# Latent rotations on GpSimd, second vectors between dense tiles, centred retention values and shorter sums in a sixteen-step transformer kernel

## The reference

```python
# layers 0 and 1 of the first block
shift_m, scale_m, gate_m, shift_f, scale_f, gate_f = split(silu(c) @ ada_w + ada_b, 6)
h = rms_norm(x, g) * (1 + scale_m) + shift_m
y = attn_hybrid_mixer(h) if layer == 0 else retention_mixer(h)
x = x + gate_m * y
...
# layer 0: 8 stick-breaking heads, 8 softmax ("moba") heads whose q and k are rotated
qm, km = rotary(q[:, 8:], pos), rotary(k[:, 8:], pos)
...
# layer 1: retention, 4 heads, dk 256, dv 512
o = (q k^T * decay) v
mu = mean(o); var = mean((o - mu) ** 2)
o = (o - mu) * rsqrt(var + 1e-5) * gn_gain
y = (silu(g) * o) @ w_o
# layers 2 and 3: h @ w_in, then a convolution branch, a latent attention of 8 heads
# (q and k normed per head and rotated), a dilated attention of 24 heads, a gated merge
```

## Time and profile before

| | us |
|---|---|
| median of 3 runs | 1530.87 |
| lowest and highest | 1525.58 and 1535.09 |
| the profiled execution | 1537.26 |
| its span, first to last instruction | 1535.5 |
| around the span | 1.8 |

### The profile page before, as it was taken

One profiled execution on the slowest core, in us unless ns is written; L12 is line 12 of the kernel. 1 busy time (PEld: TensorE's weight loads), 2 busy tenths in 40 slices (PEclk: granted clock), 3 DMA queues, 4 the chain that ended last, 5 costly groups with the idle time before them and its releaser, 6 DMA issues.

```text
span 1535.5 us, 30455 instructions
## 1 busy us (share of the span) xinstructions
PE 1492.0 (97%) x11736; PEld 1405.6 (92%) x11736; DVE 1034.7 (67%) x1821; ACT 853.2 (56%) x1438; POOL 85.5 (6%) x136
## 2 busy tenths in 40 slices
PE   8988999999999999999999999999999999999998
PEld 7777999999989999999998888889999888988998
DVE  2687688899694566555665756886666675687664
ACT  3446566544445655555565665555556666555553
POOL 0110000011000000000020000220000000021000
PEclk9999999999999999999999999999999999999999
DMA  9776488899674355565663454336666345433663
GB/s 375 264 252 191 138 274 288 287 359 334 204 275 139 111 169 161 188 185 185 190 223 122 140 163 153 111 93 183 194 189 213 108 142 171 145 97 97 193 195 122
DMA packets 81326, 292.56 MB, mean 191 GB/s; under 512 B 9200, under 2 KB 10480, under 8 KB 81088
## 3 DMA queue, kind: packets, MB, share of 16 engines
q1 hardware_dynamic: 67408, 244.03, 48.8%
q0 software_dynamic: 11792, 42.77, 8.2%
q10 hardware_dynamic: 2016, 4.21, 0.8%
HBM read 289.92 MB, written 1.05 MB: 189 GB/s over the span
## 4 chain that ended last, share of the span: by engine, by line
PE 81%; DVE 11%; ACT 4%; issue 3%; DMA 0%; SPq 0%; DVEq 0%; ACTq 0%
PE G L484 19%; PE G L485 19%; PE G L486 19%; DVE wlo L1522 4%; PE G L543 2%; PE G L545 2%; PE G L544 2%; ACT whi L1071 2%; PE G L565 1%; PE O L1017 1%; PE Tp L874 1%; PE S L986 1%; DVE aw L1530 1%; PE Tp L827 1%; PE S L600 1%
## 5 line engine op out<-in xcount | busy, mean ns | idle before, releaser
L1522 DVE TENSOR_TENSOR wlo<-raw,whi 128x1024 fp32r<-128x1024 f32 x444 | 546.7, 1233 | 309.1 <-ACT whi L1071 306.0
L484 PE MATMUL G<-h,whi 128*128 128x256 f32 x2096 | 600.2, 286 | 6.0 <-DVE at L2087 2.8
L1071 ACT ACTIVATE whi<-raw 128x1024 fp32r<-128x1024 f32 x444 | 468.7, 1057 | 241.2 <-PE G L486 179.3
L485 PE MATMUL G<-h,whi 128*128 128x256 f32 x2096 | 585.4, 279 | 0.0
L486 PE MATMUL G<-h,wlo 128*128 128x256 f32 x2096 | 585.3, 279 | 0.0
L484 PEld LDWEIGHTS G<-h,whi 128*128 128x128 f32 x2096 | 398.9, 190 | 15.3 <-issue 6.0
L485 PEld LDWEIGHTS G<-h,whi 128*128 128x128 f32 x2096 | 397.5, 190 | 1.7 <-issue 0.5
L486 PEld LDWEIGHTS G<-h,wlo 128*128 128x128 f32 x2096 | 396.9, 189 | 0.0
L1530 DVE CUSTOM_DVE_ANT_0 aw<-aw,cs,cols 128x1024 f32<-128x1024 f32 x80 | 102.3, 1279 | 0.0
L484 PE MATMUL G<-ah,whi 128*128 128x256 f32 x352 | 98.0, 278 | 0.0
L485 PE MATMUL G<-ah,whi 128*128 128x256 f32 x352 | 98.0, 278 | 0.0
(11 more groups left out here) (336 smaller groups left out, 2298.8 us busy)
## 6 DMA issues: line engine op xcount, KB each, us to landing
raw<-in_w SPq DMA_DIRECT2D x444, 512.0 KB, 3.7
aw<-in_ada POOLq DMA_DIRECT2D x80, 512.0 KB, 5.4
adaw<-in_ada SPq DMA_DIRECT2D x8, 1024.0 KB, 17.6
sn<-in_uq ACTq DMA_DIRECT2D x2, 768.0 KB, 4.4
x<-in_x SPq DMA_DIRECT2D x1, 1024.0 KB, 5.4
pt<-in_ukv ACTq DMA_DIRECT2D x2, 512.0 KB, 5.5
out<-x SPq DMA_DIRECT2D x4, 256.0 KB, 2.3
cs<-in_crow SPq DMA_DIRECT2D x1, 512.0 KB, 3.3
```

Of the source, the lines that this page charges most:

```text
L484: pe.matmul(o, wh, mv[:, 0:T], start=(k == 0), stop=False)
L485: pe.matmul(o, wh, mv[:, T:2 * T], start=False, stop=False)
L1071: act.activation(whi[:, s, :], raw[:, s, :], ACT.Copy).then_inc(w_hi, 1)
L1522: dve.tensor_tensor(wlo[:, s, :], raw[:, s, :], whi[:, s, :], ALU.subtract).then_inc(w_lo, 1)
```

## The change

1. **Rotation on GpSimd.** `rope_moba` leaves DVE. GpSimd runs the same twelve instructions between its transfers: six behind the transfer r = 5 (after b3's tile is carried off), six behind r = 9 (after b7's). PE waits for them on `mro_ready`. The transfers r = 6 to 8 now stand behind the first six, r = 10 and all later ones behind the second six.
2. **Start.** c comes as one row of 4 KB, ACT takes its silu on one partition, and PE spreads it to 128 by two matmuls of 512 columns and one row (`cs_wide`), which ACT copies to `cs` (`cs_copied`; DVE's stage loop waits for that). `x` comes ahead of `cols`. Seven small tables (780 KB) move from ACT's queue, where ACT issued them ahead of its first squares, to SyncE's, behind `adaw`. The second half's two rows and two columns are issued between the dense tiles k = 0, 1, 2, 3 of the first. The unused matmuls go from 76 to 65 (16, 2, 6, 3, 30, 8).
3. **Retention.** `v` is centred per token and head before it is used: ACT's copies of the token tiles also give row sums (`accum_out`), and DVE subtracts the mean (`centre`, at b20, 24, 28, 32: one small addition, one scalar_tensor_tensor of 128 x 1024). The mean of `o` is then zero, and the mean's matmuls, copy and subtraction go. The squares of four tiles are added by DVE to one (two instructions), so PE sums one tile, not four. Part 3 of head n moves from 36 + 4n to 35 + 4n, so none is behind b47. PE's outputs wait for `rv_ready` too.
4. **Late run.** In `run_late` the wait for the second PSUM bank stands ahead of the second tile's matmuls, no longer ahead of both.
5. **Layers 2 and 3.** The lora sums are split over j = 1 and 2, what follows is one tile later on all engines, and the heads' transposes start at j = 19 instead of 16; the last three stand among the value blocks.
6. **Head loop.** In the two steps with two dense tiles (i = 1 and i = 10) DVE carries off the first of them ahead of `minima(i)`.

The diff, cut to what the prediction speaks of:

```diff
+RET_PARTS = {}
 for _n in range(4):
-    for _part, _b in enumerate((32, 33, 34, 36)):
-        if _b + 4 * _n < 48:
-            RET_PARTS.setdefault(_b + 4 * _n, []).insert(0 if _part == 0 else 1, (_n, _part))
+    for _part, _b in enumerate((32, 33, 34, 35)):
+        RET_PARTS[_b + 4 * _n] = (_n, _part)
...
         @block.gpsimd
+            def rope_moba(n):
+                A, B = mqk[:, 4 * n:4 * n + 4:2, :], mqk[:, 4 * n + 1:4 * n + 4:2, :]
+                RA, RB = mro[:, 4 * n:4 * n + 2, :], mro[:, 4 * n + 2:4 * n + 4, :]
+                for s in range(4):
+                    pool.wait_ge(slot_free[s], 1 + n)
+                pool.tensor_tensor(RA, A, cos, ALU.mult)
+                chain.link(pool.tensor_tensor(rtmp[:, :, :], B, sin, ALU.mult))
+                chain.link(pool.tensor_tensor(RA, RA, rtmp[:, :, :], ALU.subtract))
...
                 pool.dma_start(aw[:, r % ADA_SLOTS, :], a["ada"][16 + r]).then_inc(ada_raw[r % ADA_SLOTS], 16)
+                if r in (5, 9):
+                    if r == 5:
+                        pool.wait_ge(in_att, 64)
+                    rope_moba(r // 4 - 1)
...
             def run_late(b, g, k_of, early, moving, each_k, b4=0, g4=0):
-                for m in range(2):
-                    pe.wait_ge(slot_free[(g + m - 2) % 4], taken(g + m - 2) + g4)
...
+                    if ks[0] == 0:
+                        pe.wait_ge(slot_free[(g + m - 2) % 4], taken(g + m - 2) + g4)
...
+            run_first([(0, n) for n in range(4)])
+            ada_rows(1, 0)
+            run_first([(1, n) for n in range(4)])
+            ada_cols(1, 0)
+            run_first([(2, n) for n in range(4)])
+            ada_rows(1, 1)
+            run_first([(3, n) for n in range(4)])
+            ada_cols(1, 1)
+            keep_busy(8, Tp[:, 0, :])
...
             def ret_out(hh):
                 pe.wait_ge(r_pt, hh + 1)
+                pe.wait_ge(rv_ready, hh + 1)
...
-            def ret_sum(src, sem_, n):
+            def ret_sum(hh):
                 slot = use_t()
-                pe.wait_ge(sem_, n)
-                for m in range(4):
-                    ins = pe.matmul(Tp[:, slot, 0:T], ones[:, :], sq[:, src + m, :], start=(m == 0), stop=(m == 3))
-                ins.then_inc(t_done, 1)
+                pe.wait_ge(r_added, hh + 1)
+                pe.matmul(Tp[:, slot, 0:T], ones[:, :], sq[:, 4, :], start=True, stop=True).then_inc(t_done, 1)
...
-                    if j >= 16:
-                        mla_transposes(j - 16)
+                    if j >= 19:
+                        mla_transposes(j - 19)
...
-                if b in (5, 9):
-                    rope_moba(b // 4 - 1)
...
                 for i in range(18):
+                    first = TAKEN[i][:1] if len(TAKEN[i]) > 1 else []
+                    for j in first:
+                        head_block(j)
                     if i < 16:
                         minima(i)
-                    for j in TAKEN[i]:
+                    for j in TAKEN[i][len(first):]:
                         head_block(j)
```

More of the change, by code:

```diff
@@ L97 @@
 L1_S = len(ATT_S)
-L1_T = 8 + 8
+L1_T = 8 + 4
 L1_O = 8
@@ L573, in run_two, with run_first @@
                     ins.then_inc(blk_done, 1)
-            def run_first(half):
-                tiles = [(k, n) for k in (range(0, 4) if half == 0 else range(4, 6)) for n in range(4)]
-                if half:
-                    tiles += [(k, n) for n in range(4) for k in range(6, 8)]
+            def run_first(tiles):
                 for k, n in tiles:
@@ L691, in _ @@
             pe.wait_ge(silu_c, 1)
-            for half in range(2):
-                for vec in range(2):
-                    idle = S[:, 0, :] if half == 0 else Tp[:, 0, :] if vec else O
-                    keep_busy(4, idle)
-                    ada_rows(half, vec)
-                    keep_busy(3, idle)
-                    ada_cols(half, vec)
-                keep_busy(6 if half else 22, idle)
-                run_first(half)
+            keep_busy(2, S[:, 0, :])
+            ada_rows(0, 0)
+            for n in range(2):
+                ins = pe.matmul(G[:, n, :], ones[0:1, :], cs[0:1, 512 * n:512 * n + 512], start=True, stop=True)
+            ins.then_inc(cs_wide, 1)
+            ada_cols(0, 0)
+            keep_busy(6, S[:, 0, :])
+            ada_rows(0, 1)
+            keep_busy(3, S[:, 0, :])
+            ada_cols(0, 1)
+            keep_busy(30, S[:, 0, :])
+            pe.wait_ge(cs_copied, 1)
+            run_first([(0, n) for n in range(4)])
[7 more added lines that the diff above has]
+            keep_busy(8, Tp[:, 0, :])
+            run_first([(k, n) for k in range(4, 6) for n in range(4)] + [(k, n) for n in range(4) for k in range(6, 8)])
             def sb_scores(hh):
@@ L899, in _, with lora_sums @@
                     block_u(j)
-                def lora_sums():
+                def lora_sums(tiles):
                     pe.wait_ge(csq_ready, l + 1)
-                    for tiles in ((0, 1), (2,)):
-                        slot = use_t()
-                        for k in tiles:
-                            ins = pe.matmul(Tp[:, slot, 0:T], ones[:, :], csq[:, k, :], start=(k == tiles[0]),
-                                            stop=(k == tiles[-1]))
-                        ins.then_inc(t_done, 1)
+                    slot = use_t()
+                    for k in tiles:
+                        ins = pe.matmul(Tp[:, slot, 0:T], ones[:, :], csq[:, k, :], start=(k == tiles[0]),
+                                        stop=(k == tiles[-1]))
+                    ins.then_inc(t_done, 1)
                 def rotary_key():
@@ L1128, in _ @@
                     act.activation(adrow[:, vec, :], Tp[:, vec, :], ACT.Copy).then_inc(rows_copied, 1)
+                    if half == 0 and vec == 0:
+                        act.wait_ge(cs_wide, 1)
+                        act.activation(cs[:, 0:512], G[:, 0, :], ACT.Copy)
+                        act.activation(cs[:, 512:1024], G[:, 1, :], ACT.Copy).then_inc(cs_copied, 1)
                 act.wait_ge(vec_ready, 2 * half + 2)
@@ L1776, in ret_part, with centre @@
                                       ALU.subtract).then_inc(r_lo, 1)
+            def centre(hh):
+                for g in range(G_RET + 16 + 4 * hh, G_RET + 20 + 4 * hh):
+                    dve.wait_ge(slot_free[g % 4], taken(g))
+                v = rv[:, :, 512 * hh:512 * hh + 512]
+                dve.tensor_tensor(vm4[:, hh, :], vsum[:, hh, :, 0], vsum[:, hh, :, 1], ALU.add).then_inc(rv_mean, 1)
+                dve.wait_ge(rv_mean, hh + 1)
+                dve.scalar_tensor_tensor(out=v, in0=vm4[:, hh, :].unsqueeze(2).broadcast_to([P, 2, 512]), scalar=-1.0 / 512,
+                                         in1=v, op0=ALU.mult, op1=ALU.add).then_inc(rv_ready, 1)
             dve.wait_ge(in_ret, 48)
```

176 lines of the change are left out of this document (91 added, 85 removed).

## The result

The changed kernel takes 1523.03 us, median of 14 runs (1517.17 to 1530.35), beside 1533.94 of the kernel before, 14 runs on the same chip (1525.58 to 1539.8). The ratio is 0.9929 with an interval of 0.9909 to 0.9949: 10.9 us less, inside the 1% that was called no change. The forecast was 10.8 less, 1520. The interval leaves room for anything from 7.8 to 14.0 less.

A forecast was written before the change was run, and what follows sets the result against it. PE, busy 97% of the span, was taken to bound the kernel. Terms -5.3 + 8 + 7 - 12 - 6 - 2.5 = -10.8 against the profiled 1537.26 gave 1526.5, median 1520 us, range 1496 to 1534.

The forecast's parts named there:

- the likeliest case: Whole kernel: the summed terms hold, median 1520 us, own range 1513 to 1528, chance 0.50.
- Start, -5.3: Start up to the first dense tiles: earlier sums and fewer unused matmuls save 5.3 us, bounds -2 and -7.
- Rotation, +8: First stage: rotation on GpSimd is held up by DVE and costs 8 us, bounds -7.5 and +11.5.
- the sum follows the row: First stage: GpSimd's first rotation instruction waits for DVE's whole gapless row, until 69.0; the sum takes +8.
- The working that I had put down as the rule's: First stage: GpSimd gets its turn after one DVE instruction, which makes the rotation term +4.6.
- wrong if the twelve rotation instructions last 1.1 us each: First stage, GpSimd: sign that would show the prediction wrong, twelve rotation instructions of 1.1 us each.
- The transfer r = 6 10 us or more behind r = 5: First stage, GpSimd: sign for the prediction, transfer r = 6 issued 10 us or more after r = 5.
- Retention, +7: Retention: removed sums save PE 14.3 us, but part 3 ahead of the next scores costs more; +7, bounds -12 and +9.
- Layers 2 and 3, head loop, late run, -12 - 6 - 2.5 = -20.5: Layers 2 and 3: waits at transposes and lora sums, on `at` and `cz`, and for the second bank shrink or go.
- the rotation wasn't hidden: Rival, first stage: GpSimd works between DVE's instructions or unhindered, term -7.5, 1504 us, chance 0.17.
- the retention's chain wasn't hidden: Rival, retention: ACT and DVE hide the chain of part 3, term -12, 1501 us, chance 0.18.
- the first stage didn't stay at the lower clock: Rival, b11 to b15: long PE stops keep the clock low, term 25 to 35, up to 1547 us, chance 0.10.

The follow-up runs named there:

- 9: Kernel of ret36 with the two fp32 matmuls that spread cs moved behind the first half's vectors and fewer unused matmuls ahead: 1507.76 us, 0.9831.
- experiment 3: Changed kernel with each GpSimd rotation instruction replaced by a one-operand tensor_scalar, the rotation itself left out: 1513.36 us in a single run.
- experiment 4: Changed kernel with one more bias-like GpSimd instruction behind the second rotation: 1515.38 us in a single run.
- ret36: Also called 5. Changed kernel with the retention's part 3 back at block 36 + 4n, behind the next head's decay, the last head's behind the loop: 1510.6 us, 0.987.
- ret36_sum35: Also called 6. As ret36 against the changed kernel, but PE's single sum stays at block 35 + 4n: 1518.12 us, 0.9931.
- 7: Kernel before with the retention part of the change alone: 1540.27 us, 1.0061.
- tr17: Also called 8. Changed kernel with the latent attention's transposes from tile 17 instead of 19: 1529.61 us, 1.0000.
- no_rope: Changed kernel without the first stage's rotation, scores reading the unrotated tiles: 1511.34 us, 0.9884.
- 1: Changed kernel with the first stage's twelve rotation instructions back on DVE: 1519.41 us, 0.9927.
- 10: Kernel of ret36 with the first stage's rotation on DVE and four of its 24 dots moved to steps 20 to 23: 1496.66 us, 0.9772.

## Why the prediction was right, and where it was right by luck

The total was met (-10.8 forecast, -10.9 timed, -14.3 in the profiled pair), the likeliest case was the one that came, and the start, the retention and the layers were each within 2.5 us. The first stage's rotation was off by 7, in its mechanism and not only in its size. That the timed total agrees to 0.1 us is luck: its interval is 3 us either way, and the terms of the pair add up to 3.5 us less than forecast.

- **Start, -5.3; measured -3.0.** The sums came 4.3 us sooner instead of 2.5, and the second half's part shrank by 4.9 instead of 3.3. What I had left out stood between: the clock fell to its lower level from 16.8 to 23.5, and the 60 unused records (6.9 us) ahead of the first dense tile held it to 32.31, 1.9 later than before. The pair was unlucky here: nine other traces with this start have 3.4 us of the lower clock instead of 6.8, and their b4 comes at 50.74 to 51.58, 3.6 to 4.4 sooner than before. 9 shows that little more is to be had by sooner vectors, since w's landing is next.
- **Rotation, +8; measured +0.8.** The failed step is the one that "the sum follows the row": I let GpSimd's first instruction wait for DVE's whole row until 69.0, by the 5.06 us of the earlier trace rows. It waited for one instruction. The working that I had put down as the rule's, turns one for one, gave +4.6, and the mark of the first transposes shows +4.7. What that row shows was misread: four of the seven DVE instructions in it are short ones of 0.4 us, and in the rotation's place every DVE instruction with two operands lasts 1.2. The Trainium skill, SBUF — State Buffer, section "Who interferes with whom", says that the second to issue waits until the first is finished, and that it is GpSimd's reading of SBUF at all that excludes a DVE instruction with two inputs there. The trace after agrees (2.30 us for 1.22), and so does experiment 3 with one operand (1.62); the bias instruction of experiment 4, which several DVE instructions passed, doesn't fit it. The rest, 3.8 us given back behind that mark, is clock. In the profile before, three half-clock stretches stood between the first transposes and the sum of squares, 10.2 us together; after, one, 3.4; half of the difference is 3.4 us. That was an accident of the execution and no effect of the change: the traces of ret36 and ret36_sum35, which have the same first stage, show 9.4 and 12.8 us of half clock there, and 92.3 and 94.7 us where the changed kernel has 89.8. Over the whole first stage behind b4 six traces with the rotation on GpSimd took 129.3 to 134.2 us and three with it on DVE 125.4 to 128.5, so the move costs about 4 us and not 0.8.
- Of the signs, "wrong if the twelve rotation instructions last 1.1 us each" did not come: ten lasted 2.1 to 2.3, the first of each half 1.4 and 1.5. "The transfer r = 6 10 us or more behind r = 5" did: 13.1. But the first rotation instruction didn't last many us (1.37), DVE never waited for `aw`, and PE didn't wait for `mro`; these belong to the step that failed.
- **Retention, +7; measured +6.6,** and +9.3, 4.6 either way, by itself (7). The chain was right link by link: three waits of 3.4 to 3.5 (forecast 4 to 5), four of 1.0 to 1.1 for the added squares (1.0), half clock 10.2 us, so 5.1 lost (3 x 1.7). That the clock's part came out is partly luck: with the same code and the same waits the traces show from none (tr17, stretch 120.4) to 13.7 us of half clock (no_rope, 128.1), so the term lies anywhere from +1 to +9. The order of the helpers' rows decided it: in 5 the same arithmetic without that order takes 109.7, 9.5 less than the kernel before.
- **Layers 2 and 3, head loop, late run, -12 - 6 - 2.5 = -20.5; measured -18.9.** The waits for `qk`, for `cz`, of the lora sums and of the late run went; the one for `at` fell from 2.8 to 0.7, and 1.3 for `pt` is new, both of two layers. tr17 shows the largest term by undoing it: 9.1 us in the trace and 10.9 (about 5 either way) in time, where 10.4 stood in the sum. The smaller terms have no run of their own.

The rivals: the rotation wasn't hidden (no_rope, 11 us up to the mark), the retention's chain wasn't hidden (ret36), and the first stage didn't stay at the lower clock: PE's longest wait up to the first transposes was 2.8 us and not 9.5, and it had the lower clock there for 6.8 us.

## What to carry to other kernels

Work taken from the engine that bounds is worth nothing until the chain that feeds it has been walked through the other engines' rows: 56 matmul records went, and the step that was moved one block forward with them cost more than they brought. When a wait is to be hidden, move both what waits and what stands behind it on the helper's row (5 against 6), and check with one kernel that undoes only the distance (8). GpSimd isn't a free engine beside a DVE that has no gaps: 8 us of DVE's work moved there cost DVE some 12.6 (twelve turns of 1.05; the mark came 4.7 later), where four dots moved to steps with room gave 5 (34.8 to 30.0 from b4 to the transposes, 1 against 10).

## What the runs showed of the hardware

- **PE's dense rows run at one of two cadences, at the full granted clock and without a wait.** In two stretches of 150 us inside the feed-forward stages (stretch, PE busy and records, granted clock, DMA share, GB/s), the changed kernel:

```profile
200.00:350.00 150.00, 150.00 (x1326) 1.00 0.91 312
610.00:760.00 150.00, 150.00 (x1276) 1.00 0.59 187
```

and no_rope:

```profile
200.00:350.00 150.00, 150.00 (x1276) 1.00 0.89 304
610.00:760.00 150.00, 150.00 (x1326) 1.00 0.62 194
```

113 or 118 ns a record. In the fourteen traces each of the two stages has either one, in all four combinations, with the same code in these stages; a stage takes 185.9 or 192.4 us by it (the second 197.6 or 190.8). It may be what spreads the times of one kernel (ret36: 1504.1, 1504.6, 1507.5, then 1513.7, 1514.7, 1515.3), and is why stages are compared here and not spans; in these two stages it is the same before and after. The other stages aren't free of it: the windows of 40 us under 5 (355 records and 342) lie in the retention's output weights. What sets it wasn't tried.
- **In the rotation's place GpSimd and DVE take turns one for one**, each losing the other's full length, also where GpSimd reads one operand only (1.22 us becomes 2.30, and 1.62). In one other place a GpSimd instruction was passed by several DVE instructions, short and long, before its turn (5.06, 3.85 and 2.27 us for 0.61 of work).
- **The lower clock also comes while PE is busy:** behind two fp32 matmuls of one row, in both places where they were put. All twelve traces that have them show a half clock beginning 0.4 to 1.6 us behind their end, and the two with the start of before show none there. What about them brings it wasn't tried.
